# A decoder block on one core: spatial products in full fp32, three load orders of the MLP changed, and the first norm's weights spread by TensorE

## What is computed

```python
h = rms_norm(x, norm_mix_pre)
z = h @ w_in                                   # 1024 -> 10 x 1024
y_a = a_b * causal_dwconv(a_c * a_h, conv_a_w)             # 3 taps
y_c = silu(layer_norm(causal_dwconv(c_a * sigmoid(c_g), conf_dw_w) + b))   # 31 taps
y_s = gelu(s_u) * (tril(ws) applied per head and 128-token chunk to layer_norm(gelu(s_v)) + bs)
merged = sigmoid(g_a)*(y_a @ wb0) + sigmoid(g_c)*(y_c @ wb1) + sigmoid(g_s)*(y_s @ wb2)
x = x + rms_norm(merged @ w_out, norm_mix_post)
f = square(relu(rms_norm(x, norm_ffn_pre) @ w_ff1)) @ w_ff2    # 1024 -> 4096 -> 1024
out = x + rms_norm(f, norm_ffn_post)
```

## Time and profile before

| | us |
|---|---|
| median of 3 runs | 974.44 |
| lowest, highest | 973.62, 975.53 |
| the profiled execution | 975.48 |
| its span on the chip | 973.7 |
| TensorE busy in the span | 958.7 |
| VectorE, ScalarE, GpSimd busy | 716.7, 422.6, 121.6 |

### The profile page before, as it was taken

How to read it: one execution, slowest core, us unless ns; L and a number is a source line. 1 busy time by engine, 2 the same in 40 slices (tenths; PEclk the granted TensorE clock), 3 DMA queues, 4 the chain that set the end, 5 groups by cost and what they waited for, 6 DMA issues and landing times.

```text
span 973.7 us, 13543 instructions
## 1 busy us (share of the span) xinstructions
PE 958.7 (98%) x4910; PEld 818.9 (84%) x4910; DVE 716.7 (74%) x839; ACT 422.6 (43%) x526; POOL 121.6 (12%) x146
## 2 busy tenths in 40 slices
PE   9999999999999999999999999999989999999997
PEld 7888888888888888888888888899779989989985
DVE  5458889889888898886585434598865785696698
ACT  5333332333333222223364323367735745754673
POOL 1100000001000001112200000132212112111112
PEclk9999999999999999999999999999999999999999
DMA  6323222232232222224325323469989979989765
GB/s 244 98 87 131 92 92 92 88 112 92 90 109 87 87 82 91 86 87 130 105 90 216 109 92 116 180 157 216 292 218 224 221 199 238 195 195 256 145 176 147
DMA packets 39196, 140.23 MB, mean 144 GB/s; under 512 B 4464, under 2 KB 4592, under 8 KB 39152
## 3 DMA queue, kind: packets, MB, share of 16 engines
q1 hardware_dynamic: 28608, 101.88, 30.3%
q0 software_dynamic: 9728, 34.61, 19.5%
q10 hardware_dynamic: 816, 3.15, 0.9%
HBM read 135.43 MB, written 4.19 MB: 143 GB/s over the span
## 4 chain that ended last, share of the span: by engine, by line
PE 93%; DMA 4%; DVE 1%; ACT 1%; issue 0%; POOL 0%; SPq 0%; DVEq 0%; ACTq 0%; POOLq 0%
PE ps L1449 25%; PE ps L1451 25%; PE ps L1453 25%; PE ps L1616 5%; PE ps L1620 5%; PE ps L1618 5%; DMA glu<-units_in 2%; DMA raw_d<-units_in 2%; PE ps L1523 1%; DVE w_lo L962 1%; PE ps L1492 1%; ACT w_hi L610 1%; PE ps L1557 0%; PE ps L1558 0%; PE ps L1556 0%
## 5 line engine op out<-in xcount | busy, mean ns | idle before, releaser
L1449 PE MATMUL ps<-a_hi,w_hi 128*128 128x512 f32 x576 | 225.4, 391 | 0.0
L1451 PE MATMUL ps<-a_lo,w_hi 128*128 128x512 f32 x576 | 224.2, 389 | 0.0
L1453 PE MATMUL ps<-a_hi,w_lo 128*128 128x512 f32 x576 | 224.1, 389 | 0.0
L962 DVE TENSOR_TENSOR w_lo<-raw,w_hi 128x1024 fp32r<-128x1024 f32 x124 | 153.1, 1238 | 89.2 <-ACT w_hi L610 89.0
L610 ACT ACTIVATE w_hi<-raw 128x1024 fp32r<-128x1024 f32 x124 | 130.2, 1056 | 189.8 <-PE ps L1453 119.1
L1038 DVE SCALAR_TENSOR_TENSOR conf<-glu,cols,conf (+1 forms) x240 | 187.0, 779 | 27.5 <-DVE conf L1038 26.4
L1451 PEld LDWEIGHTS ps<-a_lo,w_hi 128*128 128x128 f32 x576 | 108.2, 188 | 22.6 <-issue 0.5
L1449 PEld LDWEIGHTS ps<-a_hi,w_hi 128*128 128x128 f32 x576 | 108.1, 188 | 22.7 <-DVE w_lo L962 0.2
L1453 PEld LDWEIGHTS ps<-a_hi,w_lo 128*128 128x128 f32 x576 | 108.1, 188 | 22.5
L962 DVE TENSOR_TENSOR w_lo<-glu,w_hi 128x1024 fp32r<-128x1024 f32 x56 | 67.8, 1223 | 37.3 <-ACT w_hi L610 37.1
L1449 PE MATMUL ps<-w_hi,h_hi 128*128 128x512 f32 x224 | 88.5, 395 | 4.3 <-DVE w_lo L962 3.6
(11 more groups left out here) (175 smaller groups left out, 1663.4 us busy)
## 6 DMA issues: line engine op xcount, KB each, us to landing
raw<-units_in SPq DMA_DIRECT2D x128, 512.0 KB, 3.3
glu<-units_in POOLq DMA_DIRECT2D x40, 512.0 KB, 6.5
glu<-units_in SPq DMA_DIRECT2D x24, 512.0 KB, 5.1
raw_d<-units_in POOLq DMA_DIRECT2D x24, 512.0 KB, 7.9
raw_v<-units_in SPq DMA_DIRECT2D x16, 512.0 KB, 6.0
raw_d<-units_in SPq DMA_DIRECT2D x8, 512.0 KB, 4.0
conf<-x_in SPq DMA_DIRECT2D x4, 512.0 KB, 4.7
conf<-x_in ACTq DMA_DIRECT2D x1, 2048.0 KB, 7.8
```

The lines of the kernel that those rows point to most:

```text
L962: return nc.vector.tensor_tensor(dst, src, hi, ALU.subtract)
L1449: nc.tensor.matmul(ps[:, bank, :], left_hi, right_hi, start=first, stop=False, skip_group_check=on_top)
L1451: nc.tensor.matmul(ps[:, bank, :], left_hi, right_lo, start=False, stop=False, skip_group_check=on_top)
L1453: return nc.tensor.matmul(ps[:, bank, :], left_lo, right_hi, start=False, stop=final, skip_group_check=on_top)
```

## The change

Four things are changed.

1. The spatial products are made in full fp32: one product of ones and `ws_raw` and four of `v_tile` and `ws_raw` in place of 14 fp32r ones. The splits of v and ws fall away, but for one copy of v by ACT.
2. At the start, SP loads the norm's weight row to one partition (4 KB) ahead of x. PE makes 8 products of ones, then spreads the row with two fp32 products of 512 columns to PSUM banks 4 and 5, then makes 5 more of ones, and 4 after the turn. DVE reads the row from PSUM for the first tokens; ACT copies it to SBUF for the others, and splits the second weight unit ahead of the turned x instead of behind it.
3. In the MLP, POOL brings DOWN 5 of quarter 0 ahead of UP 4, DOWN 6 and 7 ahead of the next quarter's UP 5, and that UP 5 ahead of DOWN 4. SP waits for UP 6 instead of UP 7 ahead of the first DOWN 5, and for DOWN 6 ahead of the second quarter's UP 5.
4. In quarter 0 ACT takes the second half of UP 5 out of PSUM ahead of squaring product 1's result, no longer behind it.

```diff
-WARM, WARM_AGAIN = 20, 6
+WARM = 8, 5, 4
...
+            sp.dma_start(row[1][0:1, :], rows_d[ROW_MIX_PRE:ROW_MIX_PRE + 1, :]).then_inc(rows_loaded, 16)
             x_load(0)
-            sp.dma_start(row[0], rows_d[ROW_MIX_PRE:ROW_MIX_PRE + 1, :].to_broadcast([P, D])
-                         ).then_inc(rows_loaded, 16)
...
             for q in range(QUARTERS):
+                if q == 1:
+                    behind_sums(0, DOWN, 6)
                 if q:
...
-                        behind_sums(0, UP, {5: 7, 1: 4}[product])
+                        behind_sums(0, UP, {5: 6, 1: 4}[product])
...
                 add_block(q, UP, 7)
-                add_block(q, UP, 4)
                 if q == 0:
                     add_block(0, DOWN, 5)
+                add_block(q, UP, 4)
+                add_block(q, DOWN, 6)
+                add_block(q, DOWN, 7)
                 if q < QUARTERS - 1:
                     add_block(q + 1, UP, 5)
-                for product in (6, 7, 4):
-                    add_block(q, DOWN, product)
+                add_block(q, DOWN, 4)
...
                     split_hi(Count(0))
+                    split_hi(Count(1))
+                    turned_hi(0, 0, a_hi, 0)
                 elif c < CH - 1:
+                    if c == 1:
+                        nc.scalar.activation(row[0].rearrange("p (b n) -> p b n", b=2), ps[:, 4:6, :],
+                                             ACT.Copy).then_inc(row_ready, 1)
...
-                copy_hi(v_hi[:, :, :], by_token[:, :, bass.ds(j.times(P), P)]).then_inc(v_hi_ready, 1)
-                act.wait_ge(ws_masked, j.times(1, 1))
-                copy_hi(ws_hi[:, :], ws_raw[:, b, :]).then_inc(ws_hi_ready, 1)
+                nc.scalar.activation(v_tile[:, :, :], by_token[:, :, bass.ds(j.times(P), P)],
+                                     ACT.Copy).then_inc(v_tile_ready, 1)
...
-                act.wait_ge(joined, 5 * q + 1)
-                rectify(q, 1, "22", 1.0)
+                if q:
+                    act.wait_ge(joined, 5 * q + 1)
+                    rectify(q, 1, "22", 1.0)
                 done(q, UP, 5, 1)
                 keep(q, 5, "11", 1)
                 split_behind(q, UP, 5, 1)
+                if q == 0:
+                    act.wait_ge(joined, 1)
+                    rectify(q, 1, "22", 1.0)
...
-            keep_warm(WARM)
+            keep_warm(WARM[0])
+            pe.wait_ge(rows_loaded, 16)
+            for b in range(2):
+                mm = nc.tensor.matmul(ps[:, 4 + b, :], ones[0:1, :].bitcast(F32), row[1][0:1, b * HALF:(b + 1) * HALF],
+                                      start=True, stop=True)
+            mm.then_inc(row_spread, 1)
+            keep_warm(WARM[1])
...
-                    out = ps[:, 7, 0:P]
-                    nc.tensor.matmul(out, ones[:, :], ws_hi[:, :], start=True, stop=False)
-                    nc.tensor.matmul(out, ones[:, :], ws_lo[:, :], start=False, stop=True)
+                    nc.tensor.matmul(ps[:, 7, 0:P], ones[:, :].bitcast(F32), ws_raw[:, b, :], start=True, stop=True)
                     for c in range(CH):
-                        out = ps[:, 6, c * P:(c + 1) * P]
-                        nc.tensor.matmul(out, v_hi[:, c, :], ws_hi[:, :], start=True, stop=False)
-                        nc.tensor.matmul(out, v_hi[:, c, :], ws_lo[:, :], start=False, stop=False)
-                        mm = nc.tensor.matmul(out, v_lo[:, c, :], ws_hi[:, :], start=False, stop=True)
+                        mm = nc.tensor.matmul(ps[:, 6, c * P:(c + 1) * P], v_tile[:, c, :],
+                                              ws_raw[:, b, :], start=True, stop=True)
```

More of the change, by code:

```diff
@@ L258, in build @@
         resid = conf_flat[:, :].rearrange("p (c n) -> p c n", c=CH)
-        v_hi = sb("v_hi", [P, CH, P], F32R)
-        v_lo = sb("v_lo", [P, CH, P], F32R)
+        v_tile = sb("v_tile", [P, CH, P])
+        room = sb("room", [P, 6 * P])
         ws_raw = sb("ws_raw", [P, 2, P])
-        ws_hi = sb("ws_hi", [P, P], F32R)
-        ws_lo = sb("ws_lo", [P, P], F32R)
         bs_row = sb("bs_row", [P, 2, P])
@@ L284, in build @@
         ps = ctx.enter_context(nc.psum_tensor("ps", [P, 8, 512], F32))
-        raw_v = over("raw_v", [P, 2, D], "v_hi")
+        raw_v = over("raw_v", [P, 2, D], "v_tile")
         raw_d = over("raw_d", [P, 2, D], "conf", 2 * D)
@@ L328, in build @@
         rows_loaded = sem("rows_loaded")
+        row_spread = sem("row_spread")
+        row_ready = sem("row_ready")
         rows_again = sem("rows_again")
@@ L358, in build @@
         y_a_lo = sem("y_a_lo")
-        v_hi_ready = sem("v_hi_ready")
-        v_lo_ready = sem("v_lo_ready")
+        v_tile_ready = sem("v_tile_ready")
         ws_masked = sem("ws_masked")
-        ws_hi_ready = sem("ws_hi_ready")
-        ws_lo_ready = sem("ws_lo_ready")
         spatial_done = sem("spatial_done")
@@ L986, in turned_lo @@
                        hi[:, 4 * g:4 * g + 4, c * P:(c + 1) * P]).then_inc(act_lo_ready, 1)
-            dve.wait_ge(rows_loaded, 16)
+            two = "p (b n) -> p b n"
             for c in range(CH):
@@ L992, in _ @@
                 dve.wait_ge(rstd_ready, c + 1)
-                nc.vector.scalar_tensor_tensor(out=by_token[:, c, :], in0=resid[:, c, :],
-                                               scalar=rstd[:, c:c + 1], in1=row[0], op0=ALU.mult,
-                                               op1=ALU.mult).then_inc(normed, 1)
+                if c == 0:
+                    dve.wait_ge(row_spread, 1)
+                else:
+                    dve.wait_ge(row_ready, 1)
+                nc.vector.scalar_tensor_tensor(out=by_token[:, c, :].rearrange(two, b=2),
+                                               in0=resid[:, c, :].rearrange(two, b=2),
+                                               scalar=rstd[:, c:c + 1],
+                                               in1=row[0].rearrange(two, b=2) if c else ps[:, 4:6, :],
+                                               op0=ALU.mult, op1=ALU.mult).then_inc(normed, 1)
                 if c < CH - 1:
@@ L1078, in mix_tile @@
                 taps_own(0)
-                dve.wait_ge(v_hi_ready, j.times(1, 1))
-                lo(v_lo[:, :, :], by_token[:, :, bass.ds(j.times(P), P)], v_hi[:, :, :]).then_inc(v_lo_ready, 1)
-                dve.wait_ge(ws_hi_ready, j.times(1, 1))
-                lo(ws_lo[:, :], ws_raw[:, b, :], ws_hi[:, :]).then_inc(ws_lo_ready, 1)
                 after(u.plus(3))
@@ L1526, in _ @@
             pe.wait_ge(consts_ready, 4)
-            keep_warm(WARM)
+            keep_warm(WARM[0])
[5 more added lines that the diff above has]
+            keep_warm(WARM[1])
             pe.wait_ge(consts_ready, 5)
             turn(0, 0, 0)
-            keep_warm(WARM_AGAIN)
+            keep_warm(WARM[2])
             for c, n in V_BLOCKS:
@@ L1548, in _ @@
                         channel_unit(Count(U_MIX + PER_TILE * b + n, i, 2 * PER_TILE), a_hi, a_lo, n)
-                    pe.wait_ge(v_lo_ready, j.times(1, 1))
-                    pe.wait_ge(ws_lo_ready, j.times(1, 1))
-                    out = ps[:, 7, 0:P]
-                    nc.tensor.matmul(out, ones[:, :], ws_hi[:, :], start=True, stop=False)
-                    nc.tensor.matmul(out, ones[:, :], ws_lo[:, :], start=False, stop=True)
+                    pe.wait_ge(v_tile_ready, j.times(1, 1))
+                    pe.wait_ge(ws_masked, j.times(1, 1))
+                    nc.tensor.matmul(ps[:, 7, 0:P], ones[:, :].bitcast(F32), ws_raw[:, b, :], start=True, stop=True)
                     for c in range(CH):
-                        out = ps[:, 6, c * P:(c + 1) * P]
-                        nc.tensor.matmul(out, v_hi[:, c, :], ws_hi[:, :], start=True, stop=False)
-                        nc.tensor.matmul(out, v_hi[:, c, :], ws_lo[:, :], start=False, stop=False)
-                        mm = nc.tensor.matmul(out, v_lo[:, c, :], ws_hi[:, :], start=False, stop=True)
+                        mm = nc.tensor.matmul(ps[:, 6, c * P:(c + 1) * P], v_tile[:, c, :],
+                                              ws_raw[:, b, :], start=True, stop=True)
                     mm.then_inc(spatial_done, 1)
```

3 lines of the change are left out of this document (removed).

## The result

The changed kernel takes **998.16 us** (median of 5 runs, 995.84 to 1001.23) where the kernel before takes 975.53 (5 runs, 973.62 to 976.66). The ratio is 1.0232, with a 95% interval from 1.0215 to 1.0248. It is slower, as forecast, but by 22.6 us and not by 5.7, and it lies outside the range that the prediction gave. The profiled execution took 995.84, the fastest of the five, with a span of 994.0; that of before had a span of 973.7. So the traces account for 20.3 us; the other 2.3 are the distance of that execution from the median, and no trace shows them.

A forecast was written before the change was run, and what follows sets the result against it. TensorE, busy 958.7 of 973.7 us, was taken to bound the kernel. Terms -3.6 - 0.1 - 1.0 + 3.9 + 3.9 + 2.6 = +5.7 us took the median from 974.44 to 980.1 us; forecast's range 976 to 985.5, overall 966.0 to 985.5.

The forecast's parts named there:

- DOWN 4: MLP, quarters 0, 1 and 2: two UP 5 transfers ahead of it; -1.0, +3.9 and +3.9 us.
- Spatial gate: Eight spatial gates: full fp32 products save 0.45 us each, -3.6 us in all.
- Start: Start of the program: norm 1.0 us later, given back by earlier splits; -0.1 us in all.
- Rival (c): Start: TensorE keeps the lower clock through both products, norm at 8.6; +1.0 us, 981.1; chance 0.66 together with the forecast.
- Quarter 0, UP: Quarter 0 of the MLP: UP 4 lands at about 677.7, DOWN begins at 686.5 as before, after a 2.5 us pause.
- the loads' share: DOWN 4: SP's two loads running beside GpSimd's transfers delay it; 0.7 us taken, up to 1.9.
- The bound of 5.1: DOWN 4 of quarters 1 and 2: upper bound of the loss, +5.1 us each; the lower bound was +2.9.
- The clock: Lower clock after TensorE's pauses: 1.7 us for three of four pauses at even chances; +2.6 us, from 0 to 6.8.
- Rival (a): DOWN 4 isn't late, the two more transfers fit in: 965.4 us, partial form 969 to 974; chance 0.22 for both.
- rival (d): Gains and late DOWN 4 cancel, no clock loss, quarter 0 at its better end: 973.8 us; chance 0.08.

The follow-up runs named there:

- orders_alone: The kernel before with only GpSimd's new list and SP's new waits: 997.73 us, ratio 1.0236.
- loads_held: The changed kernel, with SP holding its two loads for UP 3 in quarters 1 to 3 until the previous quarter's DOWN 4 has landed: 989.01 us, ratio 1.0135.
- sum_first: The changed kernel with DVE's first sum of DOWN 7 ahead of the second split of DOWN 4 in quarters 0 to 2: 996.17 us, ratio 1.0228.
- start_alone: The kernel before with only the new start: 975.08 us, ratio 1.0006.

## Why the prediction was wrong

The direction and the mechanism at DOWN 4 were right; four terms of the sum were too small. By the spans the kernel lost 20.3 us where 5.7 were forecast. Of the 14.6 between, 4.9 are the clock, 5.0 quarter 0 (its UP half, and DOWN 4 behind it), 2.1 and 2.4 DOWN 4 of quarters 1 and 2, and 0.2 the gates and the start.

**Spatial gate: right.** Forecast 0.45 a gate and 1.1 us between the products on both sides. Measured: 126.73 - 125.38 less one pitch of 0.23 is 1.12 us for 1.56, that is 0.44 a gate and -3.5 in all; alone, -3.3.

**Start: nearly right in its sum, wrong in its steps.** Forecast -0.1, the norm near 7.5. The norm began at 7.04. Then the turn's eight products took 1.94 us at the lower clock (1.03 before), and the first block began at 11.71, not 10.85. The fp32 product of the earlier trace rows stood at 441.25 and is at 438.00, of which -3.5 is the gates: +0.3. The step that failed is one that the prediction takes without saying so: that the clock, once risen, stays up. Rival (c), the clock low through both products at +1.0, happened in four of nine traces: the norm then began at 9.0 (8.6 in the prediction), and the first UP product up to 2.7 us later.

**Quarter 0, UP: wrong.** The prediction has UP 4 land at about 677.7 and DOWN begin at 686.5, in times of the kernel before. In the kernel after all of this stands 3.5 us earlier, so these are 674.2 and 683.0 there; measured were 677.50 and 687.35, and that 677.50 looks like the forecast is chance. The first step that failed is the landing: 2.15 us were charged for the two transfers put ahead of UP 4. In orders_alone, which has the times of before, its second transfer was issued at 668.48 and landed at 680.59, 5.05 us behind the 675.54 of before, about two full transfers of 2.5. What part SP's earlier load of DOWN 5 has in it, no run separates. The row (start us, us, what, from that kernel's chain of waits):

```profile
668.48 12.11 DMA glu<-units_in
```

The second is the path. The pause was put ahead of DOWN, at 2.5 us; it was 4.5 us within UP, for a join behind UP 4's split, with the clock down afterwards. I had asked only when product 4 itself needs its weights, and not what else stands behind their split on DVE.

**DOWN 4: the mechanism was right, its size was not.** Two transfers ahead of it, a wait in quarters 0, 1 and 2, absent in 3: all there. In quarter 1 the wait was to be 3.9 us with the loads' share and was 5.99. By the prediction's own sum, from the first issue: 5.4 + 12.85 + 0.7 + 2.5 = 21.45; measured 813.19 - 789.70 = 23.49. The differences are +1.7 for SP's loads (2.4 for 0.7, shown by loads_held), +0.6 for the sum behind the split (shown by sum_first) and -0.3 for the pitch of the six. The bound of 5.1 was too low: it allowed 1.9 us for the loads, where 2.4 were measured, and had no term for what stands behind the split. In quarter 0 DOWN 4 was to begin at 724.5, which is 721.0 in times of the kernel after; it began at 726.04. Of these 5.0 us, 2.1 are the same terms, and 3.0 come from the wait in UP, behind which DOWN 7's first transfer was issued at 702.52 and not at 699.55.

On those 0.7 us the prediction names the page DMA: Bandwidth & Descriptors of the Trainium skill (Issuing engines are not separate DMA queues), by which the issuing engines share the same 16 engines. The trace agrees with the page here: GpSimd's last two transfers landed 3.6 and 3.8 us apart beside SP's two loads, and 2.5 apart without them. From one row, in which the loads took 5.2 us for a median of 3.3, I had read that only the loads give way. In the kernel after both give way, the loads with 9.3 us.

**The clock: the price per pause was too low, and so was the chance.** Charged were 1.7 us for three of four pauses at even chances, 2.6 in all. Every one of the four was followed by a stretch at the lower level, and three of the stretches were of 6.83 us, not 3.41: 9.2 us less the 1.7 of before, that is 7.5. The single pause of before was of 3 us; the pauses here are of 4.5 to 6.6, and with loads_held, at 3.6 to 3.9 us, the stretches were 3.41 in two quarters and 6.83 in one. So the clock's price grew with the pause, though not from one length on, and both were under-estimated together.

The sum by its own terms: gates -3.5, start and rounding 0, UP of quarter 0 +4.5, DOWN +2.3, +7.9 and +9.2 make 20.3. Rival (a) is out, since DOWN 4 is late wherever UP 5 stands between DOWN 7 and DOWN 4, and so is rival (d), since the clock fell behind every pause.

## What to carry to other kernels

When a transfer is moved later, list everything that stands behind its consumer on each in-order engine, not only its own product: a join or a sum there stops TensorE as well, and moving those moves the wait. Price a queue of accumulating transfers with the loads of other queues that run beside it, and take the upper end where a single row suggests that the queue is spared. A pause of TensorE of some 3 us or more cost more than its length in all but one case here, and several of them are to be charged in full, not at even chances. A position in a list of issues was worth 25 to 28 us here, more than all the arithmetic of the change. Take all times of a forecast from one kernel, and shift those that a gain further up shifts.

## What the runs showed of the hardware

- Accumulating transfers of 512 KB from GpSimd land 2.5 us apart when queued (2.7 to 2.8 in quarter 2 of the changed kernel), and 3.6 to 3.9 apart beside two plain loads of SP, which themselves took 9.3 us in quarter 1 in place of 3.3.
- The granted clock fell to the lower level for 3.41 or 6.83 us at every pause of TensorE of 2.6 us or more in the MLP but one (3.05 us in start_alone's trace), at times before the pause had ended (810.17, product at 813.19), at times after it. Pauses up to 1.7 us had no such stretch. With pauses of 4.7 us and more it was 6.83 us in all but one case (5.2 us in sum_first), with shorter ones 3.41 us in all but one (3.6 us in loads_held).
- With two fp32 products of one row at the start the clock fell 3.4 us behind its rise, or rose only some 8 us later, in nine traces of nine; with 128 rows in the same place it did neither in the two traces there are. That it is the single row that counts rests on these two traces, in which the order of the loads also differs; the times don't show it.
- A full fp32 product of 128 columns takes TensorE 0.11 us per record, two records a product.
